# Block products reordered so that each join reads PSUM; another opening order; four receivers for stored gate*up tiles; softplus spread over four groups

## The reference, cut to what matters

```python
def swiglu(x, w_gate, w_up, w_down):
    return (jax.nn.silu(x @ w_gate) * (x @ w_up)) @ w_down

x = x + 0.5 * swiglu(rmsnorm(x, ffn1_norm), ffn1_w_gate, ffn1_w_up, ffn1_w_down)
u = rmsnorm(x, mix_norm)
proj = u @ w_in            # lru_x | lru_y | ssd_z | ssd_xbc | ssd_dt
...                        # RG-LRU scan and SSD scan; softplus(-lru_lambda) enters the first
x = x + jnp.concatenate([lru_out, ssd_out], axis=-1) @ w_out
x = x + 0.5 * swiglu(rmsnorm(x, ffn2_norm), ffn2_w_gate, ffn2_w_up, ffn2_w_down)
# final RMSNorm
```

## Time and profile before

| what | us |
|---|---|
| three runs | 2202.66, 2204.09, 2207.38 |
| median | 2204.09 |
| profiled execution, its own time | 2212.14 |
| its span | 2210.2 |
| TensorE busy | 2140.0 |
| DVE, GpSimd, ACT busy | 1462.6, 1225.7, 593.7 |

### The profile page before, as it was taken

One profiled execution on the slowest core, in us unless ns is written; L12 is line 12 of the kernel. 1 busy time (PEld: TensorE's weight loads), 2 busy tenths in 40 slices (PEclk: granted clock), 3 DMA queues, 4 the chain that ended last, 5 costly groups with the idle time before them and its releaser, 6 DMA issues.

```text
span 2210.2 us, 36672 instructions
## 1 busy us (share of the span) xinstructions
PE 2140.0 (97%) x15504; PEld 2105.7 (95%) x15504; DVE 1462.6 (66%) x1259; ACT 593.7 (27%) x856; POOL 1225.7 (55%) x825
## 2 busy tenths in 40 slices
PE   6999999988999999899999999999999999989998
PEld 5989999988999999889999999999999999989998
DVE  7797778763222567877888596787888777642215
ACT  5211101111000224577877540122100101110003
POOL 7778888872442322325352663335988888824340
PEclk8999999999999999999999999999999999989999
DMA  4122222226321322311110422132212222363222
GB/s 146 58 77 79 76 77 97 73 101 220 96 73 58 111 93 90 120 65 51 40 60 31 173 87 89 48 116 77 69 67 97 77 77 78 108 221 90 82 58 77
DMA packets 64755, 197.84 MB, mean 90 GB/s; under 512 B 9416, under 2 KB 18120, under 8 KB 64592
## 3 DMA queue, kind: packets, MB, share of 16 engines
q1 hardware_dynamic: 63440, 194.97, 26.0%
q10 hardware_dynamic: 1152, 0.52, 0.1%
HBM read 149.37 MB, written 46.26 MB: 89 GB/s over the span
## 4 chain that ended last, share of the span: by engine, by line
PE 78%; DVE 8%; DVEq 4%; ACT 3%; DMA 2%; issue 2%; POOL 1%; POOLq 1%; ACTq 0%; SPq 0%
PE banks L770 41%; PE banks L850 30%; PE banks L1117 2%; PE banks L815 2%; DMA stage<-hidden 2%; POOLq L663 1%; DVEq L1577 1%; DMA hidden<-up 1%; DVEq L1594 1%; DVE rstd L1538 1%; DVEq L1555 1%; DVE mix L1559 0%; POOL w L664 0%; DVEq L1558 0%; DVE h_lo L1640 0%
## 5 line engine op out<-in xcount | busy, mean ns | idle before, releaser
L623 POOL TENSOR_SCALAR w_hi<-w_raw 128x1024 fp32r<-128x1024 f32 (+1 forms) x93 | 106.6, 1146 | 597.2 <-PE banks L770 531.4
L625 POOL TENSOR_TENSOR w_lo<-w_raw,w_hi 128x1024 fp32r<-128x1024 f32 (+1 forms) x100 | 270.3, 2703 | 162.2 <-DVE xbc L1886 123.4
L770 PE MATMUL banks<-h_hi,w_lo 128*128 128x344 f32 x948 | 306.2, 323 | 14.4 <-DVE x L1672 14.4
L770 PE MATMUL banks<-h_lo,w_hi 128*128 128x344 f32 x948 | 304.9, 322 | 0.0
L770 PE MATMUL banks<-h_hi,w_hi 128*128 128x344 f32 x948 | 304.8, 322 | 0.0
L770 PE MATMUL banks<-u_hi,w_lo 128*128 128x344 f32 x864 | 286.4, 331 | 6.4 <-issue 6.1
L770 PE MATMUL banks<-u_hi,w_hi 128*128 128x344 f32 x864 | 276.4, 320 | 0.0
L770 PE MATMUL banks<-u_lo,w_hi 128*128 128x344 f32 x864 | 276.0, 319 | 0.0
L1672 DVE SCALAR_TENSOR_TENSOR x<-banks,x 128x1032 f32<-128x1032 f32 x42 | 51.7, 1232 | 301.3 <-PE banks L770 301.3
L1197 ACT ACTIVATE parts<-banks 128x516 f32<-128x516 f32 x80 | 47.6, 597 | 659.1 <-PE banks L850 659.1
L770 PEld LDWEIGHTS banks<-h_hi,w_lo 128*128 128x128 f32 x948 | 180.0, 190 | 15.0 <-DVE x L1672 15.0
(11 more groups left out here) (353 smaller groups left out, 5953.4 us busy)
## 6 DMA issues: line engine op xcount, KB each, us to landing
w_raw<-in_gate_up SPq DMA_DIRECT2D x46, 512.0 KB, 4.3
hidden<-up SPq DMA_DIRECT2D x44, 516.0 KB, 6.2
stage<-hidden SPq DMA_DIRECT2D x44, 516.0 KB, 3.6
raw<-in_gate_up SPq DMA_DIRECT2D x40, 512.0 KB, 4.6
w_raw<-in_w_in SPq DMA_DIRECT2D x36, 512.0 KB, 4.2
w_raw<-in_down SPq DMA_DIRECT2D x32, 512.0 KB, 3.9
x<-in_xt SPq DMA_DIRECT2D x16, 516.0 KB, 6.6
x_kept<-x SPq DMA_DIRECT2D x16, 516.0 KB, 5.1
```

What stands on the lines that cost most here:

```text
L623: pool.tensor_scalar(w_hi[s][:, 0:n], w_raw[s][:, 0:n], 1.0, 0.0, ALU.mult, ALU.add)
L625: pool.tensor_tensor(w_lo[s][:, 0:n], w_raw[s][:, 0:n], w_hi[s][:, 0:n].bitcast(F32), ALU.subtract).then_inc(split, 1)
L770: end = pe.matmul(out[:, c, 0:CH], w[s][:, k * P:(k + 1) * P], x[kx][:, c * CH:(c + 1) * CH], start=(first and n == 0), stop=(last and n = ...
```

## The change

The order of the seven products of a group becomes p1, p2, p6, p5, p7, p3, p4 (`STEADY`), in group 0 p1, p2, p3, p6, p5, p7, p4 (`OPENING`). Only p1 is copied by ACT, each of the other six is read by DVE out of PSUM in `join`, p7 twice. The first of the two scales moves ahead of the join of p4. GpSimd's list of operands follows the order.

In the opening of FFN1 all high passes of the first pair come ahead of the low ones (`highs`, `low`), DVE makes all x_lo before the mixes, and the seven adds of squares move from GpSimd to DVE, with a third buffer for squares. The units write three banks in three chunks of 344 columns; four of 258 before. The second up tile is no more evacuated by ACT: DVE reads it from PSUM while it scales it. `norm_sum` stands ahead of step k = 6 of u1, before ahead of k = 4. Product 1 of group 0 in FFN1 waits for the root, product 2 for the read of the second up tile; in FFN2 it is products 0 and 1.

```diff
+STEADY = ("p1", "p2", "p6", "p5", "p7", "p3", "p4")
+OPENING = ("p1", "p2", "p3", "p6", "p5", "p7", "p4")
+READ = {STEADY: ("p2", "p6", "p5", "p7", "p3", "p4"), OPENING: ("p2", "p6", "p5", "p3", "p7", "p4")}
+
...
+        f1.g_at, f1.u_at = banks[:, 2:5, 0:CH], banks[:, 5:8, 0:CH]
...
+                if j >= 4:
+                    sp.wait_ge(*f.hidden.past(j - 3 if j < 8 else j - 1))
+                n, _ = stage_of(j)
+                sp.dma_start(f.stage[n][:], d.hidden[:, j, :]).then_inc(f.stage_landed[n].sem, 16)
...
+                x_again(f, src, 2)
+                if tag == "2":
+                    x_again(f, src, 7)
+                sp.wait_ge(*f.op_ready.past(7 * (NG - 1)))
+                for j in range(2, 4):
+                    load_hidden(f, j)
                 sp.wait_ge(*f.op_ready.past(NOPS))
                 for m in range(2):
                     load(("d" + tag, 0, m))
...
+                for j in range(4, 8):
...
+                sp.wait_ge(*f.done.past(NOPS))
+                x_again(f, src, 0)
+                x_again(f, src, 1)
+                sp.wait_ge(*f.hidden.past(8))
+                x_again(f, src, 5)
+                x_again(f, src, 6)
+                if tag == "2":
+                    sp.wait_ge(*f.ev.past(6 * NG))
+                    x_again(f, src, 3)
+                    x_again(f, src, 4)
+                store_hidden(f, NG // 2)
...
+                sp.wait_ge(*f.h_stored.past(32 * (NG // 2 + 1)))
+                if tag == "1":
+                    x_again(f, src, 4)
+                    x_again(f, src, 7)
...
-                if tag == "1":
-                    for k in range(1, KT):
-                        pool.wait_ge(squared["ffn1"], k + 1)
-                        if k >= 2:
-                            pool.wait_ge(added["ffn1"], k - 1)
-                        pool.tensor_tensor(f.tot[:], f.tot[:], f.c[k % 2][:], ALU.add).then_inc(added["ffn1"], 1)
...
-                    if hook and k == 4:
+                    if hook and k == 6:
...
                         before, m = divmod(o - 4, 7)
-                        if m < 2:
-                            pe.wait_ge(*f.copied.past(2 * before + m + 1))
+                        if m == 0:
+                            pe.wait_ge(*f.copied.past(before + 1))
                         else:
-                            pe.wait_ge(*f.ev.past(5 * before + m - 1))
+                            pe.wait_ge(*f.ev.past(read_number(before, order(before)[m])))
+                    elif o == (1 if f.tag == "1" else 0):
+                        pe.wait_ge(*f.rooted.past(1))
+                    if o == (2 if f.tag == "1" else 1):
+                        pe.wait_ge(*f.taken.past(4))
+                    if o == 3:
+                        pe.wait_ge(*f.mix_lo.past(4))
                     pe.wait_ge(*f.op_ready.past(o + 1))
                     w = f.op[o % RING]
                     for k in range(4):
...
-                            pe.wait_ge(*f.ev.past(5 * NG - 2 + m))
+                            pe.wait_ge(*f.ev.past(6 * NG - 1 + m))
...
+            def highs(unit, out, k):
...
                 pe.wait_ge(x_hi_done, k + 1)
-                for n, (w, x) in enumerate(((w_hi, f1.bh), (w_lo, f1.bh), (w_hi, f1.bl))):
...
+                for n, w in enumerate((w_hi, w_lo)):
+                    for c in range(CHUNKS):
+                        pe.matmul(out[:, c, :], w[unit][:, k * P:(k + 1) * P], flat(f1.bh[k])[:, c * CH:(c + 1) * CH],
+                                  start=(k == 0 and n == 0), stop=False)
+
+            def low(unit, out, k):
+                pe.wait_ge(x_split, k + 1)
+                for c in range(CHUNKS):
+                    end = pe.matmul(out[:, c, :], w_hi[unit][:, k * P:(k + 1) * P], flat(f1.bl[k])[:, c * CH:(c + 1) * CH],
...
             for k in range(AHEAD):
-                as_it_comes(g, gate, k)
+                highs(g, gate, k)
             for k in range(AHEAD):
...
-                as_it_comes(u, up, k)
+                highs(g, gate, k)
+                highs(u, up, k)
+            for k in range(KT):
+                low(g, gate, k)
+            for k in range(KT):
+                low(u, up, k)
...
+            def part(f, q):
+
+                act.wait_ge(*f.done.past(7 * q + 1))
                 if q:
-                    act.wait_ge(*f.ev.past(5 * (q - 1) + (2, 4)[n]))
-                act.activation(halved(f.p[n][:]), twos[o % 4], ACT.Copy).then_inc(f.copied.sem, 1)
+                    act.wait_ge(*f.ev.past(6 * q - 1))
+                act.activation(halved(f.p[:]), twos[7 * q % 4], ACT.Copy).then_inc(f.copied.sem, 1)
...
             for k in range(KT):
                 first_high(k)
-                if k >= AHEAD - 1:
...
+            act.wait_ge(*f1.mix_ready.past(1))
+            taken(f1, ("u1", 0), f1.u_at, f1.u[0])
+            for k in range(2, 4):
+                mix_high(f1, k)
+            for k in range(4, KT):
+                first_square(k)
             act.wait_ge(consts, 1)
-            plain_pair(f1)
+            act.wait_ge(squared["ffn1"], KT)
+            second_pair(f1)
...
             def plain_pair(f):
-                dve.wait_ge(*f.taken.past(8))
                 for tile in f.g:
                     last = dve.tensor_tensor(tile[:], tile[:], rstd[:], ALU.mult)
                 last.then_inc(f.scaled.sem, 1)
-                for tile in f.u:
-                    dve.tensor_tensor(tile[:], tile[:], rstd[:], ALU.mult)
+                dve.tensor_tensor(f.u[0][:], f.u[0][:], rstd[:], ALU.mult)
+                dve.wait_ge(used, U(("u" + f.tag, 1)) + 1)
+                dve.tensor_tensor(cut(f.u[1][:]), f.u_at, cut(rstd[:]), ALU.mult).then_inc(f.taken.sem, 1)
                 hidden_pair(f, 0)
...
             def corners(f, q, between=None):
+                last = q == NG - 1
                 dst = f.u if q % 2 else f.g
+                c11, c12, c21 = dst[0][:, 0:HT], dst[0][:, HT:T], dst[1][:, 0:HT]
+                c22, part = dst[1][:, HT:T], f.p[:]
+
+                def join(name, a, to, second=None):
+                    o = number(q, name)
+                    dve.wait_ge(*f.done.past(o + 1))
+                    dve.drain()
+                    end = dve.tensor_tensor(halved(to), twos[o % 4], halved(a), ALU.add)
+                    if second:
+                        end = dve.tensor_tensor(halved(second[1]), twos[o % 4], halved(second[0]), ALU.add)
+                    end.then_inc(f.ev.sem, 1)
+                    if between and name in between:
+                        between[name]()
...
+                dve.wait_ge(*f.copied.past(q + 1))
+                join("p2", part, c11)
+                join("p6", part, c21)
+                join("p5", c21, part)
+                if q == 0:
+                    join("p3", part, c12)
+                join("p7", part, c22, (c21, c21))
+                if q:
+                    join("p3", part, c12)
+                dve.drain()
+                if not last:
+                    dve.tensor_tensor(dst[0][:], dst[0][:], rstd[:], ALU.mult)
+                return lambda: join("p4", c21, c21)
+
...
+            def last_corner(f, q, finish):
                 dst = f.u if q % 2 else f.g
-                dve.wait_ge(*f.done.past(7 * q + 7))
-                dve.tensor_tensor(halved(dst[1][:, 0:HT]), twos[(7 * q + 6) % 4], halved(f.p[3]), ALU.add).then_inc(f.ev.sem, 1)
-                dve.drain()
-                dve.tensor_tensor(dst[0][:], dst[0][:], rstd[:], ALU.mult)
+                finish()
+                if q == NG - 1:
+                    for j in range(6, 8):
+                        hidden_low(f, j)
+                    dve.tensor_tensor(dst[0][:], dst[0][:], rstd[:], ALU.mult)
+                dve.drain()
                 dve.tensor_tensor(dst[1][:], dst[1][:], rstd[:], ALU.mult).then_inc(f.scaled.sem, 1)
                 if q % 2:
                     hidden_pair(f, q // 2 + 1)
...
             def groups(f, extra):
+                lows = {"p2": lambda: hidden_low(f, 0), "p6": lambda: hidden_low(f, 1),
+                        "p5": lambda: (hidden_low(f, 2), hidden_low(f, 3)), "p7": lambda: hidden_low(f, 4),
+                        "p3": lambda: hidden_low(f, 5)}
...
+                    finish = corners(f, q, lows if q == NG - 1 else None)
...
                 first_low(f1, k, V_FFN1, x_hi_done, x_split)
-                if k >= 4:
-                    mixes(f1, k - 4, V_FFN1)
+            for k in range(4):
+                mixes(f1, k, V_FFN1)
+            for k in range(1, KT):
+                dve.wait_ge(squared["ffn1"], k + 1)
+                dve.drain()
+                dve.tensor_tensor(f1.tot[:], f1.tot[:], f1.c[k % 3][:], ALU.add).then_inc(added["ffn1"], 1)
             for k in range(4):
                 mix_low(f1, k)
...
+            groups_and_down(f1, {1: prepare_start, 2: lambda: prepare_series((15, 13, 11, 9)), 3: lambda: prepare_series((7, 5, 3)),
```

(5 more changed lines are left out.)

281 lines of the change are left out of this document (104 added, 177 removed).

## The result

| | before | after |
|---|---|---|
| first comparison, median | 2204.03 (4 runs, 2202.66 to 2207.38) | 2168.16 (4 runs, 2166.82 to 2169.42) |
| last comparison, median | 2210.60 (9 runs, 2206.12 to 2214.95) | 2168.96 (4 runs, 2168.09 to 2172.62) |
| ratio, first and last | | 0.9835 [0.9818, 0.9852], 0.9812 [0.9798, 0.9825] |
| profiled execution: own time, span | 2212.14, 2210.2 | 2169.42, 2167.6 |

The change makes the kernel 36 to 42 us faster, depending on which runs of the kernel before it is set against; 42.6 us by the two profiled executions. The forecast of 2163 (2143 to 2188) holds.

A forecast was written before the change was run, and what follows sets the result against it. The prediction took TensorE, busy 97% of the span, as the bound, with other engines mattering only where they stop it. Stage terms summed to −41.3 us from 2212.14, or 2170.8; less 8.05 this gave 2163 us, range 2143 to 2188.

The forecast's parts named there:

- What bounds: Whole kernel: TensorE busy 97% of the span; the change aims at six lines of its waits, 56.3 us.
- Opening of FFN1: FFN1's start and first groups: x_lo waits go, a new 8.9 us wait comes; net −16 us (−22 to −10).
- sixteen mix ops of 0.77 to 34: DVE in the opening of FFN1: sixteen mix ops of 0.77 us each, done by 34 us.
- seven adds of 1.3: DVE in the opening of FFN1: seven adds of squares, 1.3 us each, done by 43.3 us.
- the prediction's two signs of being wrong: Waits for p2's join recurring in each even group, or the reciprocal in FFN1's opening starting after 62 us.
- Softplus: FFN1's early even groups: series terms and steps stop TensorE some 1.3 and 1.9 us, where before 0.6 was lost.
- Steady groups: Even groups: DVE reads p2 in time by 0.5 to 2.4 us; 0 change for 36 groups.
- Ends: Last groups of both FFNs, fewer waits for joins and residuals: FFN1 −11.5 us (−9 to −16), FFN2 −15.5 (−12 to −16.5).
- T1+28.3: End of FFN1: last pair made 28.3 us after T1, the end of the last group but one.
- the step "−1": Between lx and z: moving the scale of z 0 ahead of one decode step gains 1 us (0 to 8).
- The sum −41.3: Whole kernel: stage terms −16, −11.5, −1, +2.7 and −15.5, taken from the profiled 2212.14 us, giving 2170.8.
- "The same distance": Sum to median: the profiled execution lay 8.05 us above the median 2204.09; the same was assumed after the change, giving 2163.

The follow-up runs named there:

- Experiment 7: Changed kernel with two receivers for all stored tiles, loads of tiles 2 to 7 behind the first two weight loads; 2187.2 us.
- 10: Changed kernel with the lows of tiles 0 to 3 ahead of the last group's joins, four receivers kept; 2166.8 us.
- experiments 2 and 3: First: changed kernel with the scale of z 0 moved back, 2167.6 us. Second: kernel before with only that scale moved ahead, 2209.6 against 2211.5.
- experiment 4: Changed kernel with ScalarE evacuating the second up tile and the norm sum ahead of k = 4, both as before; 2166.2 us.
- 8: Changed kernel with ScalarE evacuating the second up tile, norm sum at k = 2, and in FFN1 four tiles summed on TensorE, four adds on DVE; 2163.3 us.
- 11: Changed kernel with the five softplus, history and step pieces after the first in groups 3, 5, 7, 9, 11 instead of 2 to 6; 2166.0 us.
- 6: Changed kernel with softplus whole in group 1, history in group 2 and steps in group 3; 2176.1 us.

## Why the forecast held, step by step

- **What bounds.** Right: 97% of the span was TensorE, and the gain is its waits and the slow stretches behind them. Six lines of the earlier trace rows held 56.3 us; 8.2 remain in them (1.4, 1.4 and 5.4 for joins), and 21.5 are new, for up 1 and for low weights. Of the 42.6 us, 26.7 are idle time of TensorE and 15.9 its busy time. Three chunks for four are 2.1 of the latter by the prediction's estimate; the rest fits the granted clock, whose mean over the span rose from 0.984 to 0.993.
- **Opening of FFN1: the mechanism right, two terms mis-sized.** The wait for up 1 came where forecast, 10.6 us and not 8.9, ending at 77.05 and not 72.4; the restart was 2.6 (34.37 us for 264 matmuls of 120.2 ns). The terms: "sixteen mix ops of 0.77 to 34", of which three took 5.8 beside GpSimd's weight splits and ended at 37.9; "seven adds of 1.3", which took 11.2, the first beside a split. The four weight sums took 4.0 and not 2.9. mix_low was 10.9 for 13.3; GpSimd, waiting for weights until 50.39, came in behind its start, and that this is the reason is argued. With all this the reciprocal started at 64.13 and not 59.5: that is past 62, one of the prediction's two signs of being wrong, and it was a true sign for this stage: its gain was 6.4 us smaller, while the total held. The first pair ended at 35.7, not 33.0, with two waits of 1.3 and 1.8 for GpSimd's low weights; this seems to have cost nothing, DVE being later still. Group 1 ended at 114.3, where 109.0 was forecast.
- **Softplus.** Pieces in groups 2, 4 and 6 stopped TensorE 1.3 us each; I had 1.3 and 1.9 in two of them and none for the short end piece of group 4.
- **Steady groups.** Right. The read of p2 follows the end of the group by 12.6 us and is over at 13.2 (p4's join at 441.92, p2's at 454.17, below), where 14.4 was the limit.

```profile
441.92 0.69 DVE L1623 TENSOR_TENSOR up<-banks,up 128x516 f32<-128x516 f32 x1
...
454.17 1.48 DVE L1623 TENSOR_TENSOR gate<-banks,part 128x516 f32<-128x516 f32 x2
```

- **Ends.** FFN1 gave more than forecast: the last pair's store and load, 3.92 and 5.38 us below against 3.97 and 6.53 in the earlier trace rows, left d0,2 a wait of 0.3 us, and no restart. FFN2 is within 1.3 us; its wait was 1.1, where under 1 was forecast. The prediction's terms behind T1+28.3 add up to T1+42.4, not 43.5 to 46.5; what it put on top has no row, so that the measured T1+44.1 lies between them is luck (the pair was done at T1+30.0). Experiment 7 shows the receivers, with the early loads, to be the cause of some 17 of the 30 us, and 10 that with four of them the place of the lows isn't one. The other 13 are not taken apart: lows ahead of the joins with only two receivers, and a store with fewer loads ahead of it, stand as untested parts.

```profile
492.18 3.92 DMA hidden<-up
...
496.97 5.38 DMA stage<-hidden
```

- **z: the step "−1" failed.** The reason I gave for a small gain was right (the set waited for is that of z 1), and the move gave next to nothing (experiments 2 and 3). What I left out is that DVE was late there by stretches beside GpSimd, and that these could change with the rest of the program: 6.3 us, 4.7 of the wait and 1.6 of the restart behind it (4.48 us for 27 matmuls, 6.07 before). That the forecast's range took it in ("0 to −8") is luck: it was not this that it was made for.
- **From the sum to the median: failed.** The sum −41.3 met −42.5 by luck, as misses of opposite signs: +6.4, −4.2, −5.3, +0.6, +1.3. "The same distance" of 8.05 us put the forecast 5 us low; without it 2170.8 would have stood against 2168.2 and 2169.0.
- **The pages.** "VectorE: DVE Perf Modes" of the Trainium skill, TRN2 errata table, would have joins from PSUM take longer than sums in SBUF: the trace disagrees, 0.69 or 0.70 for each. (The prediction's 0.45 us a group by that table counts seven joins; five joins read PSUM before, so it is two more, 0.13 us.) "SBUF — State Buffer", Who interferes with whom, agrees in the main: joins from PSUM stayed at 0.69 to 0.70, and the long instructions that were stretched have two SBUF inputs, the rows at 904.95 above among them. But a short one with a single SBUF input was stretched too: DVE's TENSOR_SCALAR on `lam` at 103.77 took 1.18 us for 0.16, beside a GpSimd split that ended at 104.92. The page's rule for one SBUF input, as it stands, excepts the modes that use two ports, which the prediction left out; whether this instruction ran in one, no trace shows. The 2.5 ns a matmul of "TensorE: Matmul & The Clock Gate", Back-to-back issue gap, is by that section the gap of a single matmul apart, not of a stream with weight loads as here; the rows have 12.7 and 13.4 ns over the columns at 2.4 GHz, for 258 and 344 columns.

## What to carry to other kernels

When several engines feed the one that bounds, move a wait on paper to the end of the longest chain: freeing a bank early (experiment 4) gained only 2 to 3 us where the chain through DVE was the bound, and shortening that chain at the bounding engine's expense, in its idle time (8), gained 3 more. Small serial pieces belong in the iterations that have slack, which the idle time before each join shows (11), and three waits of 1.3 us cost 3.9 us in all, while two of 3.5 cost over 10, since the clock was low behind them (6). And take the noise of the reference from repeated runs: a profile 8 us above three timed runs was the ordinary case for this kernel, not a stray.

## What the runs showed of the hardware that I had not expected

Where DVE's first instruction started 0.35 us ahead of GpSimd's, GpSimd was stretched, and where they started together, DVE: DVE's pair of two-input instructions took 3.1 us in one order and 5.4 in the other, and the GpSimd instruction beside them 1.79 for 1.05. The kernels with the first form waited 5.0 to 6.1 us some 23 us later, those with the second 1.4; each kept its form in every trace looked at. That the one causes all of the other is argued from the order of the rows and not tried, and why DVE starts 0.35 us later in the kernel before is open. The kernel before spread over 2202.1 to 2215.1 us over the four comparisons; the changed one over 2166.8 to 2172.6 in two.
